# Sixteen more tokens routed by indirect DMAs, the last two pairs' rows fetched amid the stage, and a smaller staging buffer

## What is computed

```
expert (i, j):  activation = gelu(x . u[i, j])        u, v: 16384 rows of 1024 numbers
layer output of a token = sum over 8 heads, 16 chosen experts of  weight * activation * v[i, j]
```

## Time and profile before

| what | us |
|---|---|
| median of 3 runs | 1613.78 |
| lowest, highest | 1613.72, 1616.48 |
| the profiled execution's own time | 1613.47 |
| its span, first to last instruction | 1611.7 |
| PE busy | 1581.9 |
| DVE busy | 1251.7 |
| ACT busy | 922.1 |
| POOL busy | 474.4 |
| granted TensorE clock, mean of the span | 0.995 |

### The profile page before, as it was taken

One profiled execution on the slowest core, in us unless ns is written; L12 is line 12 of the kernel. 1 busy time (PEld: TensorE's weight loads), 2 busy tenths in 40 slices (PEclk: granted clock), 3 DMA queues, 4 the chain that ended last, 5 costly groups with the idle time before them and its releaser, 6 DMA issues.

```text
span 1611.7 us, 28335 instructions
## 1 busy us (share of the span) xinstructions
PE 1581.9 (98%) x9931; PEld 1382.7 (86%) x9931; DVE 1251.7 (78%) x2489; ACT 922.1 (57%) x1670; POOL 474.4 (29%) x336
## 2 busy tenths in 40 slices
PE   9999999999999999999999998999999999999998
PEld 8999899999988888777777766988888888788886
DVE  7888879878987777777777775778777876687777
ACT  5766655555466665555555554665555546555554
POOL 1000001878778862455555560110000000000000
PEclk9999999999999999999999998999999999999999
DMA  7666756777777776999999994446556653355553
GB/s 240 235 232 229 249 178 194 189 183 191 186 190 184 178 193 194 307 340 335 339 332 346 334 382 164 129 137 198 187 188 194 197 171 130 127 181 188 193 186 104
DMA packets 124433, 347.94 MB, mean 216 GB/s; under 512 B 35248, under 2 KB 37040, under 8 KB 123952
## 3 DMA queue, kind: packets, MB, share of 16 engines
q1 hardware_dynamic: 87408, 294.93, 55.2%
q0 software_dynamic: 32000, 42.06, 10.1%
q10 hardware_dynamic: 4928, 9.64, 1.7%
HBM read 331.31 MB, written 14.75 MB: 215 GB/s over the span
## 4 chain that ended last, share of the span: by engine, by line
PE 84%; issue 8%; DVE 4%; DMA 2%; ACT 1%; POOL 1%; SPq 0%; POOLq 0%; DVEq 0%
PE ps L1443 16%; PE ps L1425 9%; PE ps L1426 9%; PE ps L1427 9%; PE ps L1445 8%; PE ps L1488 7%; PE ps L1609 7%; PE ps L1490 6%; PE ps L1492 6%; PE ps L1622 2%; DMA raw<-in_v_tab 1%; PE ps L1600 1%; PE ps L1459 1%; DVE low L1934 1%; DVE held_low L1934 1%
## 5 line engine op out<-in xcount | busy, mean ns | idle before, releaser
L1934 DVE TENSOR_TENSOR low<-raw,high 128x1024 fp32r<-128x1024 f32 (+1 forms) x516 | 621.5, 1209 | 145.7 <-ACT high L982 135.8
L982 ACT ACTIVATE high<-raw 128x1024 fp32r<-128x1024 f32 (+1 forms) x517 | 538.7, 1045 | 281.8 <-PE ps L1427 130.1
L1443 PE MATMUL ps<-x_parts,high 128*128 128x512 f32 x1184 | 420.1, 398 | 0.0
L1425 PE MATMUL ps<-x_parts,low 128*128 128x256 f32 x1328 | 377.9, 285 | 1.2 <-DVE x_parts L2053 1.2
L1427 PE MATMUL ps<-x_parts,high 128*128 128x256 f32 x1328 | 375.7, 283 | 0.0
L1426 PE MATMUL ps<-x_parts,high 128*128 128x256 f32 x1328 | 375.7, 283 | 0.0
L1445 PE MATMUL ps<-x_parts,low 128*128 128x256 f32 x1184 | 331.8, 280 | 0.0
L871 POOL DMA_INDIRECT routed<-h_tok,subln x128 | 265.2, 2072 | 140.1 <-DVE h_tok L2319 67.9
L1443 PEld LDWEIGHTS ps<-x_parts,high 128*128 128x128 f32 x1184 | 222.3, 188 | 52.5
L1425 PEld LDWEIGHTS ps<-x_parts,low 128*128 128x128 f32 x1328 | 254.7, 192 | 3.0 <-DVE low L1934 1.1
L1426 PEld LDWEIGHTS ps<-x_parts,high 128*128 128x128 f32 x1328 | 254.7, 192 | 0.0
(11 more groups left out here) (387 smaller groups left out, 2159.0 us busy)
## 6 DMA issues: line engine op xcount, KB each, us to landing
raw<-in_u_tab SPq DMA_DIRECT2D x128, 512.0 KB
raw<-in_v_tab SPq DMA_DIRECT2D x128, 512.0 KB
raw<-in_ffn_in SPq DMA_DIRECT2D x88, 512.0 KB
raw<-in_w_mix SPq DMA_DIRECT2D x56, 512.0 KB
raw<-in_ffn_out SPq DMA_DIRECT2D x44, 512.0 KB
routed<-arena POOLq DMA_DIRECT2D x16, 512.0 KB, 3.9
raw<-in_w_query SPq DMA_DIRECT2D x16, 512.0 KB
h_tok<-routed SPq DMA_DIRECT2D x32, 256.0 KB
```

Source lines behind the costliest of these rows:

```text
L982: a.activation(w_high(p, 0, n), cols(raw, p, 0, n), ACT.Copy).then_inc(slot_high[p.slot], 1)
L1425: pe.matmul(dst, left[1], right[0], start=start, stop=False)
L1443: pe.matmul(bank(b).rearrange("p (h t) -> p h t", h=2), cols(high, p, k * PARTS, PARTS), both[:, k], start=(k == 0), stop=False)
L1934: v.tensor_tensor(w_low(p, 0, n), cols(raw, p, 0, n), w_high(p, 0, n).bitcast(F32), ALU.subtract).then_inc(slot_low[p.slot], 1)
```

## The change

1. `ROUTED` goes from 128 to 144, so `GROUPS` goes from 16 to 12. The second token tile's 16 extra tokens do not fill the partitions of a scatter. So SP writes their indices and weights to device memory (`repacked`) and reads them back with 8 slots of 16 tokens on the 128 partitions, and POOL issues 16 more indirect DMAs (`scatter_extra`), two at a time, from head 5 on.
2. `routed` has 144 columns for each j: it is zeroed by 18 DMAs instead of 16, its blocks are 288 KB instead of 256 KB, and DVE's `weigh` covers 144 columns. DVE forms the extra indices in each round, and waits for `packed_out` before the second group's one-hots.
3. `stage` holds 4 pieces instead of 8 (`DUMP`), so there are twice as many dumps of half the size. ACT and DVE no longer wait for `dumped` before the first coefficients of the outer stage.
4. Rows of pairs 30 and 31 are fetched after the coefficients of pairs 22 and 26 (loop index 20 and 24) instead of last, with a semaphore (`late_rows`) and windows (`late_windows`, in `stage`) of their own.
5. The end of the outer stage is reordered on PE, ACT and DVE: the rest products come first, then pairs 28 and 29, the turn of the first tile, and pairs 30 and 31. DVE does `add_rest` before `add_fetched`.

The diff, cut to its core:

```diff
-ROUTED = PARTS
+EXTRA = 16
+SPREAD = PARTS // EXTRA
+OF_HEAD = 16 // SPREAD
+ROUTED = PARTS + EXTRA
...
-DUMP = 8
+DUMP = 4
...
-ZERO_PARTS = 16
+ZERO_PARTS = 18
...
+            by_place = repacked.rearrange("(q t) (a n) -> a t q n", t=EXTRA, a=2)
             for k in range(EARLY, NKEYS):
+                if k == EARLY + 10:
+                    sp.wait_ge(chosen_ready, ROUNDS)
+                    for a in range(2):
+                        sp.dma_start(by_place[a], by_spread[a][GATHERED:GATHERED + EXTRA]).then_inc(packed_out, 16)
+                if k == EARLY + 12:
+                    sp.wait_ge(packed_out, 32)
+                    sp.dma_start(params[:, 64:64 + 2 * EXTRA], repacked).then_inc(packed_in, 16)
                 load(piece_u(k), u_tab[k])
...
                     sp.wait_ge(scattered, 16 * SLOTS)
+                    sp.wait_ge(scattered_extra, 16 * EXTRA)
...
+            def scatter_extra(h):
+
+                if h >= 1:
+                    pool.wait_ge(scattered_extra, 16 * OF_HEAD * h)
+                for n in range(OF_HEAD * h, OF_HEAD * (h + 1)):
+                    pool.indirect_dma_start(entries, bass.IndirectOffsetOnAxis(ap=packed_index[:, n:n + 1], axis=0),
+                                            packed_weight[:, n:n + 1], None, compute_op=ALU.add).then_inc(scattered_extra, 16)
...
-                scatter(h)
+                if h < 5:
+                    scatter(h, 0, 16)
+                    continue
+                if h == 5:
+                    pool.wait_ge(packed_in, 16)
+                scatter_extra(2 * (h - 5))
+                scatter(h, 0, 8)
+                scatter_extra(2 * (h - 5) + 1)
+                scatter(h, 8, 16)
+            scatter_extra(6)
+            scatter_extra(7)
...
                 gather_acts(n + 2)
-                pool.wait_ge(pair_mixed, n + 1)
-                gather_rows(n + 2)
+                if n + 2 < PAIRED - LATE_PAIRS:
+                    pool.wait_ge(pair_mixed, n + 1)
+                    gather_rows(n + 2)
                 coefficients(n + 2)
+                if n in (20, 24):
+                    gather_rows(PAIRED - LATE_PAIRS + (n - 20) // 4)
...
                 if p == PAIRS - 1:
-                    a.wait_ge(dumped, 16 * (NKEYS // DUMP - 1))
                     coef_high_part(0)
...
                     one_hots(0)
+                    v.wait_ge(packed_out, 32)
                     one_hots(1)
```

More of the change, by code:

```diff
@@ L960, in norm @@
                 if k == 2:
-                    a.wait_ge(pair_mixed, PAIRED)
-                    a.activation(moved[0:GATHERED, D:D + HALF], bank(7)[GATHERED:PARTS, :], ACT.Copy).then_inc(moved_ready, 1)
+                    for half in range(2):
+                        a.wait_ge(tile_done[1], 2 * (k - 1) + half + 1)
+                        a.activation(moved[GATHERED:PARTS, half * HALF:(half + 1) * HALF], bank(2 + half)[0:GATHERED, :], ACT.Copy).then_inc(moved_ready, 1)
                 evacuate_turned(k_turn, (0,), gain)
@@ L1624, in rows_product @@
                 ins.then_inc(pair_mixed, 1)
[L1626 to L1627 removed]
+            after = {12 + 8 * m: (2 * m, 2 * m + 1) for m in range((PAIRED - LATE_PAIRS) // 2 - 1)}
             def outer_step(j):
@@ L2311, in _ @@
                 chain.step(v.tensor_scalar(first_place[:, 0:32], slot_j[:, 0, heads], float(ROUTED), token, ALU.mult, ALU.add))
+                chain.step(v.tensor_scalar(first_place[:, 32:64], slot_j[:, 1, heads], float(ROUTED), token_extra, ALU.mult, ALU.add))
                 v.wait_ge(exp_ready, it + 1)
@@ L2406, in _, with add_rest @@
             lower, upper = slice(0, GATHERED), slice(GATHERED, PARTS)
+            def add_rest():
+                v.wait_ge(c_ready, PAIRED)
+                v.wait_ge(pair_mixed, PAIRED - LATE_PAIRS)
+                for half in range(2):
+                    h = h_tok[upper, D + half * HALF:D + (half + 1) * HALF]
+                    v.wait_ge(tile_done[1], 2 + half + 1)
+                    chain.step(v.tensor_tensor(h, h_back[upper, D + half * HALF:D + (half + 1) * HALF], bank(2 + half)[upper], ALU.add))
+                    v.wait_ge(moved_ready, 1 + half)
+                    chain.wait()
+                    v.tensor_tensor(h, h, moved[upper, half * HALF:(half + 1) * HALF], ALU.add)
             def add_fetched():
```

96 lines of the change are left out of this document (50 added, 46 removed).

## The result

The changed kernel takes 1624.49 us, median of 4 runs (1621.83 to 1625.74); the kernel before took 1614.53 beside it (4 runs, 1613.72 to 1616.48). The ratio is 1.0059 with a 95% interval of 1.0043 to 1.0075: slower by 0.6%. The profiled execution is the lowest of the four, 1621.83 us with a span of 1620.0; the kernel before had 1613.47 and 1611.7. The forecast was 1620.6 for the profiled execution, in 1611 to 1629; it measured 1.2 us more, and the median 3.9 us more.

The account below looks back on a forecast made before the run. PE, busy 98% of the span, was taken as the bound. Late outer-stage start +15.2, clock +2.5, stage's end -11.1 and added DMA traffic +0.5 gave +7.1 us on 1613.47: 1620.6 us, range 1611 to 1629.

Parts of the forecast that it names:

- What bounds the kernel: Whole kernel: PE busy 98% of the span; POOL's 30 us free not all usable, since loads of `routed` wait for scatters.
- Part 1: Inner stage: four one-hot groups fewer save PE 1.8 us, reaching the end only if the outer stage can start earlier.
- Part 2: Inner stage: sixteen more scatters at 2.23 us move POOL's last scatter end from 612.5 to 642.4.
- Landing: After POOL's last scatter: it lands 3.4 us later, at 645.8, and SP issues the loads of `routed` at 646.0.
- What waits behind it: Start of outer stage: 11.5 us from loads to PE's first product plus 1.3 for row gathers; start at 658.8, +15.2 us.
- The clock: Start of outer stage: PE's 18 us idle brings half clock for 5 us afterwards, costing +2.5 us, bounds 0 to 5.
- Part 4: Within the outer stage: two pairs' rows and wider `routed` blocks add 3.1 MB of DMA, +0.5 us, between 0 and 6.2.
- Part 3: End of outer stage: with the new order, second tile's turn at 975.8 instead of 986.85, -11.1 us, bounds -9 to -12.
- (c): Outer stage: DMA engines become the bound, row gathers delaying piece 1 by 6 us and rows costing 4; 1628.8 us, chance 0.17.
- (b): Start of outer stage: scatters stay hidden, needing POOL's end 13 us sooner; start 3.0 us earlier, 1599.9 us, chance 0.08.
- (a): Inner stage: cheap extra scatters at 1.535 us each, POOL ends 6.3 us sooner; 1612.5 us, no measurable change, chance 0.13.

Follow-up runs that it names:

- e2: The changed kernel with eight extra scatters instead of sixteen (136 routed tokens, fourteen groups): 1602.54 us, ratio 0.9928 to the kernel before.
- e1: The changed kernel without its sixteen extra scatters (128 routed tokens, sixteen groups): 1606.41 us, ratio 0.9954 to the kernel before.
- e8: The changed kernel with 165 idle products on PE in the wait before the outer stage: 1638.45 us, ratio 1.0144 to the kernel before.
- e7: The changed kernel without extra scatters and with the old order at the outer stage's end, early fetch kept: 1605.72 us, ratio 0.9941 to the kernel before.
- e10: The changed kernel without extra scatters, rows of pairs 30 and 31 fetched last, old order of the end: 1612.35 us, ratio 0.9979 to the kernel before.
- e9: The changed kernel with 80 idle products on PE before the wait ahead of the outer stage: 1619.75 us, ratio 1.0033 to the kernel before.
- e3: The changed kernel with SP's loads of pieces 1 to 3 of `v` ahead of its wait for the scatters: 1615.61 us, ratio 1.0003 to the kernel before.
- e4: The changed kernel with the rows of pairs 30 and 31 fetched last again, new order kept: 1621.35 us, ratio 1.0041 to the kernel before.
- e5: The changed kernel with eight extra scatters, late fetch of pairs 30 and 31, and pieces 1 to 3 of `v` loaded ahead of SP's wait: 1602.18 us, ratio 0.9924.
- e6: The changed kernel with eight extra scatters and the rows of pairs 30 and 31 fetched last: 1604.22 us, ratio 0.9938 to the kernel before.
- e11: The changed kernel with each DVE `low` of the inner stage done as two half-size instructions: 1603.73 us, ratio 0.9939 to the kernel before.
- e12: The kernel before with each DVE `low` of the inner stage done as two half-size instructions: 1614.34 us, ratio 0.9991 to the kernel before.

## Why the prediction was right, and where its terms were off

The terms stand in the order of the prediction. The sum was +7.1 us; by the profiled execution the terms are 14.4 + 1.4 + 1.4 - 9.3, +7.8 before rounding, and the span grew by 8.3. That the sum came so near is in part luck: the late start and the clock were priced 0.8 and 1.1 us too high, the stage and the end 0.9 and 1.8 us too low, and the four errors leave 0.7.

- **What bounds the kernel** held: the loads of `routed`, not POOL's next use, set how much of POOL's 30 free us counted. e2 shows the free part, and e1 against the changed kernel (0.0105 of 1614, 17 us) shows the price once it is spent.
- **Part 1, fewer groups**: right that it is hidden, mis-sized by half. I read the eight products at 0.89 us in the earlier trace rows as two groups. The count is of instructions, and e8 shows two for each fp32 product, so it is one group. PE came to the end of the inner stage at 638.51 (658.03 - 19.52), 3.65 us sooner than before (642.16), not 1.8. The wait took it whole. In e2, with two groups fewer and no wait, it shows: PE starts at 640.02, where e1, with all groups, was ready at 641.76 (642.21 less its wait of 0.45).
- **Part 2, the scatters' end**: predicted 642.4, measured 642.95. The sum is right by errors that cancel. The scatters were longer than the mean I took: the 64 old ones 2.043 us instead of 1.934 and the sixteen new ones 2.086, 9.4 us in all. Against that the new wait was 1.78 instead of 3.1 us, head 4 began at 452.64 and so 0.8 us sooner, not 0.5 later, and two pauses that I had passed over in the trace before didn't come again, 6.7 us beyond the usual 0.30 (one of 0.95 us did). POOL's timeline of the kernel before has them:

```profile
576.07 1.54 POOL L871 DMA_INDIRECT routed<-h_tok,subln  x1 [3.48 <-issue]
...
594.93 1.54 POOL L871 DMA_INDIRECT routed<-h_tok,subln  x1 [3.80 <-issue]
```

  What they waited for no row tells. They stand before the same two scatters, the 114th and the 121st, in e1, e7 and e10 (2.9 to 3.7 us), so they seem to belong to the place in POOL's program; in e9 the changed kernel's program had neither, in e3, e4 and e8 the first of the two with 1.6 to 2.7 us. And the step "the extra ones are of the same form and stand among those" took a mean where there are two kinds: what counts is how many scatters start inside a `low` and how much of it is left. The long ones rose from 32 of 64 to 44 of 80, and their mean from 2.32 to 2.47 us.
- **Landing**: 1.47 us from the last scatter's end to SP's issue (644.42), not 3.6 (3.4 for the landing and 0.2 for SP). So the figure in the Trainium skill, some 2.0 us fixed ("DMA: Bandwidth & Descriptors", "Anatomy of one DMA — SWDGE (gpsimd) path"), was nearer here than my rows. In other places of these runs the wait from a scatter's end to the next scatter behind its landing is 1.6 to 4.8 us: 1.6 to 1.9 before the last pair where there are sixteen, 2.8 to 3.3 before the last one in e2, e5 and e6, 2.6 to 4.8 after a head of sixteen. What makes it long or short stays open.
- **What waits behind it**: 13.6 us from the loads to the first product (658.03 - 644.42), predicted 12.8. The load of piece 1 took 7.22 us against 5.99, so 1.2 us more, where I had 1.3 for the crowd of row gathers. That the gathers are the cause is argued: the load took 7.2 to 7.3 us in the changed kernel, e4 and e9, where they start beside it, and 5.5 to 6.5 us in the kernel before, e1, e2, e10, e11 and e12, where they come later. The other steps took 6.4 us where my sum had 5.5: of the 1.2 us that I took off for the dump's wait, 0.3 came. e3 shows the queue's part.
- **The clock**: 1.4 us, predicted 2.5. The first piece took 3.75 us instead of 2.37 (643.64 to 646.01), and at 662 the granted clock was full again, 4 us after work began; I had carried over the 5 us after the stalls of the old end and priced all of it. e8 and e9 show the same 1.4 on the first piece, but not a stage that ends sooner by it, so this term and the next can't be told apart by the runs.
- **Part 4, the stage**: +1.4 us up to piece 124, predicted 0.5, as much as one wait of 1.37 us for `v_rows`, of which the earlier trace rows have none. e6 removes it, without gain.
- **Part 3, the end**: -9.3 us from piece 124's start to the second turn (31.23 before, 21.90 now), predicted -11.1. The step that fell short is DVE's part. It was busy with `low`s and coefficients almost without a pause from 973.10 to 979.28, so `add_experts` began 6.72 us after piece 124's start (972.76), where my sum has 5.2, and from there the scaling took 5.5 us to come, not 5.1. All that follows is 1.3 to 2.0 us late. DVE's timeline there:

```profile
978.05 1.23 DVE L1980 TENSOR_TENSOR low<-raw,high 128x1024 fp32r<-128x1024 f32 x1
979.48 1.29 DVE L2456 TENSOR_TENSOR h_tok<-arena,ps 128x512 f32<-128x512 f32 x2 [0.21 <-DMA arena<-in_rows]
...
984.99 1.41 DVE L2485 SCALAR_TENSOR_TENSOR h_tok<-h_tok,stats,arena 128x512 f32<-128x512 f32 x2 [0.69 <-POOL stats L866]
```

  The credit was also given to the wrong part: I worked out the gain by the reordering, line by line. e7, with the old order and the early fetch, has it nearly whole (a stage of 336.75 us), as has e4, with the new order and the late fetch (336.68).

**The rivals.** (c), the DMA engines as the bound, did not come: PE waited 1.4 us for rows, not 4, and piece 1's load took 1.2 us longer, not 6. (b) is what e2 shows with eight scatters, 1602.54 where I had worked out 1599.9 for it. Its condition was too mild: POOL's end 13 us sooner would not have hidden the scatters. In e2 SP's loads had to leave at 628.91, 17 us before the 646.0 of my sum. (a), cheap scatters, deserved more thought than its 0.13, not for this kernel, where it did not come, but for its mechanism. I named the rule of the Trainium skill ("GPSIMD Engine Reference", "Specifications") that GpSimd and VectorE contend for SBUF when VectorE reads two inputs there, applied it to the one-hots and found it small. The operation that mattered was the `low`, 128 x 1024 with two inputs, which runs beside POOL in the whole stage. e11 makes the scatters cheap by way of the `low`, all eighty and not only the extra ones: at 1.65 us each they are hidden, as in (b), and the kernel takes 1603.73.

## What to carry to other kernels

Before giving a queue more work, ask how much of its free time ends at a wait that others share: here 30 us looked free, eight more scatters cost nothing and the next eight 21 us (ratios 1.0059 and 0.9928, with two more groups of one-hot tokens gone). Loads that need nothing from a wait belong ahead of it. And where a group's shortest and longest instruction lie far apart, don't take the mean but sort the instances by what the other engines did at their start. Here that led to a remedy worth 19 us where the outer stage waited for the scatters (e11), and nothing where it did not (e12).

## What the runs showed of the hardware

- An indirect DMA of 128 numbers costs GpSimd 1.54 us, and when it starts t us into VectorE's `low` (fp32, 128 x 1024, both inputs in SBUF) it costs 1.54 + (1.10 - t) (80 scatters of the changed kernel). VectorE's `TENSOR_REDUCE` from PSUM of 1.0 us and `low`s that begin 0.3 us or more after the scatter's start leave it at 1.54 to 1.55 in that stage. The one-hots' two-input operation (128 x 512, 0.69 us) lengthens it as well: in the kernel before, a scatter that starts 0.27 us into one takes 1.82 us (463.90). The Trainium skill ("SBUF — State Buffer", "SBUF: two separate sides") describes an exclusive lock on a shared pair of ports, held for the whole instruction, and for a VectorE operation with two SBUF inputs only against a GpSimd operation that reads SBUF; that fits the trace's straight line, and e11, where two half-size instructions let GpSimd in between. It does not explain all: the longest scatter of the changed kernel, 3.15 us at 304.52, starts 0.76 us into a two-input operation (`L2310`, 128 x 1024), has a `low` right behind that, and is 1.6 us over the 1.54, where the first has only 0.34 left; there GpSimd did not get in between. That `low`s starting later don't lengthen a scatter is this trace's own addition. Ports as the cause are argued from the fit; which part of the scatter needs them no run here tells.
- In the inner stage GpSimd's scatters fell into step with VectorE, in patterns that repeat, such as two short and three long (1.54, 1.54, 2.44, 2.43, 2.51). The same program's last scatter ended 7.8 us apart in five executions, 8.3 us of spread being there already at head 4's first scatter (444.33 to 452.64).
- TensorE's granted clock went to 0.50 (1.2 GHz) when it stood idle for 19.5 us and was back at 1.00 (2.4 GHz) by 662, 4 us after work began; with idle products in the gap it stayed at 1.00, and the piece behind it took 2.4 us instead of 3.75.
- A 128 x 128 fp32 product shows as two instructions, 0.224 us together.
